# Delta scan of a two-layer block: other orders for block loads, block products, copies and query-decay loads

## What is computed

```python
def gated_delta_chunked(q, k, v, g, beta, s0):
    # S_t = a_t (I - b_t k_t k_t^T) S_{t-1} + b_t k_t v_t^T,  o_t = S_t^T q_t
    ...
    kb = k * beta[..., None]
    m = jnp.where(strict, jnp.einsum('bhnid,bhnjd->bhnij', kb, k) * decay, 0.0)
    a = m + jnp.eye(c, dtype=F32)
    rhs = jnp.concatenate([v * beta[..., None], kb * jnp.exp(g)[..., None]], axis=-1)
    sol = lax.linalg.triangular_solve(a, rhs, left_side=True, lower=True, unit_diagonal=True)
    ...
    def step(s, xs_n):
        v_new = u_n - jnp.einsum('bhck,bhkv->bhcv', w_n, s)
        o_n = jnp.einsum('bhck,bhkv->bhcv', qg_n, s) + jnp.einsum('bhij,bhjv->bhiv', attn_n, v_new)
        s = s * gl_n[..., None, None] + jnp.einsum('bhck,bhcv->bhkv', kd_n, v_new)
        return s, o_n
```

## Time and profile before

| | us |
|---|---|
| median of three runs | 2071.34 (2070.23 to 2074.94) |
| the profiled execution: its own time | 2068.77 |
| the profiled execution: span from the first instruction to the last | 2066.1 |
| TensorE busy | 1891.9 (92% of the span) |
| VectorE busy | 616.7 (30%) |
| ScalarE busy | 431.5 (21%) |
| GpSimd busy | 69.0 (3%) |

### The profile page before, as it was taken

One profiled execution on the slowest core, in us unless ns is written; L12 is line 12 of the kernel. 1 busy time (PEld: TensorE's weight loads), 2 busy tenths in 40 slices (PEclk: granted clock), 3 DMA queues, 4 the chain that ended last, 5 costly groups with the idle time before them and its releaser, 6 DMA issues. The chain is left out here.

```text
span 2066.1 us, 23949 instructions
## 1 busy us (share of the span) xinstructions
PE 1891.9 (92%) x9336; PEld 1040.5 (50%) x9336; DVE 616.7 (30%) x1351; ACT 431.5 (21%) x864; POOL 69.0 (3%) x102
## 2 busy tenths in 40 slices
PE   6999998899999899999899988889999898999997
PEld 3436455896878543332333333323333245767775
DVE  1476555256621211111111111110111223432223
ACT  3222640327231111100111111100111022521011
POOL 1000410100000000000000000000000000000000
PEclk9999999899999899999999999999999999999999
DMA  9444347306383879999999999999999772124442
GB/s 366 163 163 155 141 103 200 87 13 207 83 289 123 346 318 427 428 429 429 428 429 428 429 429 428 429 428 429 428 428 429 304 281 93 62 71 156 149 155 99
DMA packets 97251, 567.12 MB, mean 274 GB/s; under 512 B 32992, under 2 KB 41952, under 8 KB 66080
## 3 DMA queue, kind: packets, MB, share of 16 engines
q1 hardware_dynamic: 94880, 560.69, 68.2%
q10 hardware_dynamic: 2304, 5.51, 0.9%
HBM read 555.02 MB, written 11.14 MB: 274 GB/s over the span
## 5 line engine op out<-in xcount | busy, mean ns | idle before, releaser
L2087 PE MATMUL expert_gb<-expert_ring,hT 128*64 128x512 f32 x768 | 199.7, 598 | 44.6 <-DMA expert_ring<-in_w_gu_units 44.6
L1975 DVE TENSOR_SCALAR hT<-expert_gb 128x512 f32<-128x512 f32 x32 | 22.1, 692 | 682.7 <-PE expert_lb L2087 682.7
L2087 PE MATMUL expert_lb<-expert_ring,hT 128*64 128x512 f32 x768 | 197.4, 592 | 0.0
L2136 PE MATMUL expert_yb<-expert_ring,hT 128*64 128x512 f32 x384 | 167.4, 592 | 0.0
L2136 PE MATMUL expert_yb<-expert_ring,h2T 128*64 128x512 f32 x384 | 167.4, 592 | 0.0
L478 PE MATMUL mix_in_pj<-hT,mix_in_pj_ring 128*128 128x512 f32 (+1 forms) x384 | 143.3, 532 | 1.3 <-DVE hT L598 1.3
L2493 PE MATMUL attend_bank<-hT,expert_ring 128*128 128x256 f32 x640 | 141.4, 379 | 0.0
L2493 PEld LDWEIGHTS attend_bank<-hT,expert_ring 128*128 128x128 f32 x640 | 121.6, 190 | 25.1 <-issue 9.6
L2087 PEld LDWEIGHTS expert_gb<-expert_ring,hT 128*64 128x64 f32 x768 | 51.1, 136 | 155.4 <-DMA expert_ring<-in_w_gu_units 79.4
L2026 ACT ACTIVATE hT<-hT 128x512 f32<-128x512 f32 x32 | 20.2, 631 | 513.2 <-DVE hT L1975 513.2
L150 PE MATMUL delta_scan_fill_bank<-hT,fill_w 128*128 128x512 f32 (+1 forms) x288 | 102.3, 514 | 9.3 <-DMA fill_w<-in_w_fill 6.6
(11 more groups left out here) (483 smaller groups left out, 2589.8 us busy)
## 6 DMA issues: line engine op xcount, KB each, us to landing
expert_ring<-in_w_gu_units SPq DMA_DIRECT2D x96, 2048.0 KB, 29.0
expert_ring<-in_w_down_units SPq DMA_DIRECT2D x48, 2048.0 KB, 32.3
tail<-in_w_gu_units SPq DMA_DIRECT2D x16, 2048.0 KB, 30.5
late<-in_w_gu_units SPq DMA_DIRECT2D x16, 2048.0 KB, 29.0
mix_in_wm<-in_w_mod_units SPq DMA_DIRECT2D x11, 2048.0 KB, 9.4
expert_ring<-in_w_up_units SPq DMA_DIRECT2D x22, 1024.0 KB, 6.2
late<-in_w_down_units SPq DMA_DIRECT2D x8, 2048.0 KB, 34.4
tail<-in_w_down_units SPq DMA_DIRECT2D x8, 2048.0 KB, 35.3
```

The lines of the kernel that those rows point to most:

```text
L1975: v.tensor_scalar(glu, gb[j][:], LIMIT, None, ALU.min).then_inc(s_glu, 1)
L2087: m = pe.matmul(b[halves[h], :], xT[:, k, x], unit[z][:, r0 + c0 + 512 * h:r0 + c0 + 512 * h + 512], start=False, stop=(k == KT - 1))
L2136: m = pe.matmul(yb[h][halves[j], :], hidT[j][:, c, hh * SLOTS:(hh + 1) * SLOTS], unit[z][:, r0:r0 + 512], start=False, stop=(f == 7))
```

## The change

- The mask blocks of direction 1 are stored and loaded back by ScalarE's queue (`store_m(act, 1)` after four of the eight `ktok` copies, `load_m(act, 1)` after all of them); those of direction 0 stay on SP.
- VectorE finishes direction 0 (line 1005, then line 1008) before direction 1.
- The 14 loads of turned blocks get three semaphores per direction and another order: two blocks of `tl` for each direction (`s_x1`), two diagonal blocks of `tt` for each (`s_x2`), then one of `tl` and two of `tt` for each (`s_x3`). y5 waits for the first, d5 for the second, y6 for the third.
- ScalarE issues filler load `f + 2` ahead of copy `f` for products 10 to 15. SP issues loads 18 to 21 and stores 16 to 19 behind the block loads.
- Filler 16 stands behind e5 on TensorE, 17 behind y6, 18 and 19 behind d6.
- e5, y6 and d6 issue one product of direction 0 and one of direction 1 in turn. The lists in `USES` follow.
- The copies of y5 move to VectorE. Those of y6 and d6 are split: ScalarE takes y6 of direction 0 and d6 of direction 1, VectorE the others.
- The two query-decay loads stand ahead of filler store 17 and load 19, after both directions' y6; their Exp stands behind ScalarE's copies of scan step 0.

The diff, cut:

```diff
-    TLB = ((0, 1, 2), (3, 2, 1))
+    TLB = ((0, 2, 1), (3, 1, 2))
+    TTB = ((1, 3, 0, 2), (2, 0, 3, 1))
...
-    for kind in ("y5", "d5", "e5"):
+    for kind in ("y5", "d5"):
         USES += [(kind, d, c) for d in d2 for c in range(2)]
+    USES += [("e5", d, c) for c in range(2) for d in d2]
     for kind in ("y6", "d6"):
-        USES += [(kind, d, t) for d in d2 for t in range(NTILE)]
+        USES += [(kind, d, t) for t in range(NTILE) for d in d2]
...
+        def store_m(eng, d):
+            for g in g2:
+                copied(eng, ("kg", NTILE - 1, g))
+            for b in range(NB):
+                eng.dma_start(A.block_m[d]...[b], tt[d]...[quad(b), :, quad(b)]).then_inc(s_bs[d], 16)
+        def load_m(eng, d):
+            eng.wait_ge(s_bs[d], 16 * NB)
+            eng.dma_start(bm[d]..., A.block_m[d]).then_inc(s_bl, 16)
+        def store_blocks(eng, d):
+            eng.wait_ge(s_sub[d], NSUB + 1)
+            eng.dma_start(A.block_t[d], xt[d]...).then_inc(s_xs[d], 16)
+            eng.wait_ge(s_sub[d], NSUB + 2)
+            eng.dma_start(A.block_tt[d], xx[d]...).then_inc(s_xs[d], 16)
+        def low(eng, d, b, sem):
+            eng.dma_start(tl[d]...[quad(b), :, LC[d, b]:LC[d, b] + BLK], A.block_t[d]...[b]).then_inc(sem, 16)
+        def diagonal(eng, d, b, sem):
+            eng.dma_start(tt[d]...[quad(b), :, quad(b)], A.block_tt[d]...[b]).then_inc(sem, 16)
...
 # SP
                     if f == 5:
-                        (the stores and loads of block_m for both directions)
+                        store_m(sp, 0)
+                        load_m(sp, 0)
-                    if f == 11:
-                        (stores; then for each d four loads into tt, three into tl)
-                for f in range(F1 - 2, F1):
-                    S.fill.store(sp, f)
-                    S.fill.load(sp, f + 2)
+                for d in d2:
+                    store_blocks(sp, d)
+                for d in d2:
+                    sp.wait_ge(s_xs[d], 32)
+                    for b in TLB[d][0:2]:
+                        low(sp, d, b, s_x1[d])
+                for d in d2:
+                    for b in TTB[d][0:2]:
+                        diagonal(sp, d, b, s_x2[d])
+                for d in d2:
+                    low(sp, d, TLB[d][2], s_x3[d])
+                    for b in TTB[d][2:]:
+                        diagonal(sp, d, b, s_x3[d])
+                S.fill.load(sp, 18)
+                S.fill.store(sp, 16)
                 for d in d2:
                     copied(sp, ("y6", d, NTILE - 1))
                     sp.dma_start(qg[d]..., A.decay_rows[d, 2:4]...).then_inc(s_qr[d], 16)
+                for f in range(17, F1):
+                    S.fill.load(sp, f + 2)
+                    S.fill.store(sp, f)
...
 # ScalarE
                 for t in range(NTILE):
+                    if t == 2:
+                        store_m(act, 1)
                     (two copies of ktok)
-                for f in range(6, 18):
+                load_m(act, 1)
+                for f in range(6, 16):
+                    if f >= 10:
+                        S.fill.load(act, f + 2)
                     copy_fill(f)
                     if f >= 10:
                         S.fill.store(act, f)
-                        S.fill.load(act, f + 2)
-                (copies of y5; copy_fill(18))
-                for d in d2:
-                    for c in range(2):
+                for c in range(2):
+                    for d in d2:
                         (copy of e5 (d, c))
-                copy_fill(19)
-                (copies of y6 of both directions; qg: wait and Exp)
+                copy_fill(16)
+                (copies of y6 of direction 0)
+                copy_fill(17)
+                (copies of d6 of direction 1)
+                copy_fill(18)
+                copy_fill(19)
                 for n in range(NTILE):
                     (copies of vn)
+                    if n == 0:
+                        for d in d2:
+                            act.wait_ge(s_qr[d], 16)
+                            act.activation(qg[d], qg[d], ACT.Exp).then_inc(s_qe[d], 1)
...
 # VectorE
                 for d in d2:
                     (line 1005)
-                for d in d2:
                     (line 1008)
+                (copies of y5 of both directions)
                 (copies of d5 of both directions)
-                (copies of d6 of both directions)
+                (copies of y6 of direction 1)
+                (copies of d6 of direction 0)
...
 # TensorE
-                for f in range(6, 18):
+                for f in range(6, 16):
                     fill(f)
                 pe.wait_ge(s_z, 1)
                 for d in d2:
-                    pe.wait_ge(s_xl[d], 16 * (NB + len(TLB[d])))
+                    pe.wait_ge(s_x1[d], 32)
                     (y5)
-                fill(18)
                 for d in d2:
+                    pe.wait_ge(s_x2[d], 32)
                     (d5)
-                for d in d2:
-                    for c in range(2):
-                        (e5 of direction d, half c)
-                fill(19)
+                for c in range(2):
+                    (e5 of both directions, half c, one product of each in turn)
+                fill(16)
                 for d in d2:
+                    pe.wait_ge(s_x3[d], 48)
                     copied(pe, ("e5", d, 1))
-                    (y6 of direction d, four tiles)
+                (y6: four tiles, one product of each direction in turn)
+                fill(17)
                 for d in d2:
                     copied(pe, ("d5", d, 1))
-                    (d6 of direction d, four tiles)
+                (d6: four tiles, one product of each direction in turn)
+                fill(18)
+                fill(19)
```

More of the change, by code:

```diff
@@ L1122, in _ @@
                         m.then_inc(fullsem(("d5", d, c)), 1)
-                for d in d2:
-                    f, x = PAIRS[d][0]
-                    for c in range(2):
-                        take(pe, ("e5", d, c))
-                        for a in range(16 * c, 16 * c + 16):
-                            t, h = a // HA, a % HA
-                            m = pe.matmul(flat(TURN["e5", d, c][0])[quad(x), BLK * (a % 16):BLK * (a % 16) + BLK],
-                                          tt[d][quad(x), t, h, quad(x)], y5s[d][quad(x), a, :], start=True, stop=True)
-                        m.then_inc(fullsem(("e5", d, c)), 1)
@@ L1132, in _ @@
-                fill(19)
-                for d in d2:
-                    copied(pe, ("e5", d, 1))
-                    for t in range(NTILE):
-                        b = take(pe, ("y6", d, t))
-                        for h in range(HA):
-                            m = pe.matmul(flat(TURN["y6", d, t][0])[SECOND[d], 64 * h:64 * h + 64],
-                                          tt[d][FIRST[d], t, h, SECOND[d]], tl[d][FIRST[d], t, h, :], start=True, stop=True)
-                        m.then_inc(fullsem(("y6", d, t)), 1)
+                for c in range(2):
+                    for d in d2:
+                        take(pe, ("e5", d, c))
+                    last = [None, None]
+                    for a in range(16 * c, 16 * c + 16):
+                        t, h = a // HA, a % HA
+                        for d in d2:
+                            f, x = PAIRS[d][0]
+                            last[d] = pe.matmul(flat(TURN["e5", d, c][0])[quad(x), BLK * (a % 16):BLK * (a % 16) + BLK],
+                                                tt[d][quad(x), t, h, quad(x)], y5s[d][quad(x), a, :], start=True, stop=True)
+                    for d in d2:
+                        last[d].then_inc(fullsem(("e5", d, c)), 1)
@@ new lines, in _ @@
+                fill(16)
+                for d in d2:
+                    pe.wait_ge(s_x3[d], 48)
+                    copied(pe, ("e5", d, 1))
+                for t in range(NTILE):
+                    for d in d2:
+                        take(pe, ("y6", d, t))
+                    for h in range(HA):
+                        for d in d2:
+                            last[d] = pe.matmul(flat(TURN["y6", d, t][0])[SECOND[d], 64 * h:64 * h + 64],
+                                                tt[d][FIRST[d], t, h, SECOND[d]], tl[d][FIRST[d], t, h, :], start=True, stop=True)
+                    for d in d2:
+                        last[d].then_inc(fullsem(("y6", d, t)), 1)
```

90 lines of the change are left out of this document (42 added, 48 removed).

## The result

Measured: 2060.23 us (median of 5, 2057.91 to 2062.49) against 2074.94 us for the kernel before beside it (2070.23 to 2077.76). The ratio is 0.9934, 95% interval 0.9919 to 0.9949: faster, by 0.66%. The forecast was 2046 in a range of 2039 to 2058: the measured time lies 14 us above it, outside the range.

The account below looks back on a forecast made before the run. The delta-scan stretch from filler 15 to step 0 was taken as bound by TensorE and its waits. Products 31.2, waits 4 and clock 3 made 38.2 us against 62.40, 24.2 less, giving 2046 us (range 2039 to 2058).

Parts of the forecast that it names:

- The sum's waits and its clock: Filler 15 to step 0: waits 4 us (bounds 1 and 9), clock loss 3 us (0 and 7), beside 31.2 of products.
- The first two land at 342 + 1.8 + 2.6 = 346.4 ... I take 347: Loads ahead of y5: each direction's first two `tl` blocks land at 347, between 346.4 and 350.
- y5 waits beyond 352: Sign at y5's start: waiting past 352 would prove the prediction wrong; y5 was expected at 346 to 349.
- One stretch like the 6.83 us one costs half of it; I take 3: TensorE's clock among the short products: one half-clock stretch costs 3 us, bounds 0 and 7.
- Low clock all along: Rival, y5 to filler 16: clock falls at the first wait and stays down, 6 us more, 2052 us; chance 0.08.
- Mask blocks on two queues: Mask blocks ahead of VectorE's column phase: direction 1 on ScalarE's queue gains 1 us, bounds nothing and 1.4.
- Alternation: e5, y6, d6: alternating directions' corners takes e5 to 1.9 us and halves y6 and d6 from 14.95 to 7.5.
- No overlap: Rival at y6, d6, e5: alternation does nothing for 64x64 corners, 9 us of gain lost, 2055 us; chance 0.12.
- Slower: Rival at y6 and d6: switching corners drains, 218 ns a product, 55.8 us together, total time of 2094 us; chance 0.03.
- Copies on VectorE, filler loads, query decays: y5 copies covered but about 1 us; filler loads hidden; query-decay loads cost 0.5 us wait, their Exp free.
- Loads stay slow: Rival ahead of y6: loads keep 1.8 us each, land at 369, y6 waits 6 to 7 more, 2053 us; chance 0.12.

Follow-up runs that it names:

- the best trace: Changed kernel with mask blocks on SP's queue, `block_t` stored first, filler steps behind y5/d5 halves (three first, two second) and four behind e5: 2046.67 us, 0.9868.

## Why the prediction was wrong, step by step

- **The sum's waits and its clock were wrong, its work somewhat low.** In the best trace, with the clock up and the wait covered, the stretch takes 36.34 us, near the forecast 38.2, but that is luck: it holds 35.08 us of work and 1.26 of idling, where the sum had 31.2 of work, 4 of waits and 3 of clock. By the starts of its rows the short products take 11.4 us there (predicted 9.3), y6 and d6 7.6 (7.5) and the fillers, three of them cut up, 16.1 (14.4).
- **"The first two land at 342 + 1.8 + 2.6 = 346.4 ... I take 347"** failed: y5 starts at 355.65, outside 346.4 to 350; 3.0 us of that are the later last mask product, so it is 5.7 us late (+67.8 against +62.1), and filler 15 ends 2.1 us sooner (+59.3 against +61.4), which lengthens the wait. Only 1.3 of the 5.7 is the issue (+58.4 against +57.1); the rest is the landing, 9.3 us in place of 4.4. The 1.8 us is a mean over 14 loads, and no pace for the first two: in the trace of before too, its first two loads landed 7.5 us behind the first issue (343.83 to 351.30). What shares the engines was shown to count: 3.7 us less idling without two of the filler loads, 3.3 with the `block_tt` stores moved behind, of which 1.8 is the earlier issue. "y5 waits beyond 352" was named as what would prove the prediction wrong, and did.
- **"One stretch like the 6.83 us one costs half of it; I take 3"** failed as a size, and its upper bound of 7 too: 10.6. The rival *Low clock all along* had the mechanism and nearly the numbers (9.3 + 1.9 forecast, 8.6 + 2.05 measured); its 2052 and the 7.5 us of wait that it did not have make 2059.5. It was given 0.08 because d5 had run at full clock for all its 4.05 us, but that was right behind 5.07 us of filler, and the change takes that filler away. That row spoke for the rival as much as against it.
- **The two failed terms do not add up as repairs.** Each repair of the wait alone gave nothing at step 0: the time won went into the stops behind it (d5's 3.64 us, or 2.40 and 1.17) and into filler 16, 0.5 to 0.7 us longer at half clock. With three steps of filler among the short products the earlier loads do reach step 0 (+102.3 against +105.5).
- **Mask blocks on two queues**, a gain of 1 us (0 to 1.4): a loss of about 1.2 at the column phase. The rule quoted there from the Trainium skill, that a second issuing engine saves issue time alone, was nearer than the bound taken from the DMA share.
- **Alternation** was right: y6 and d6 3.95 us each against 3.75, and with directions in turn only by tile the run is 8.8 us slower. *No overlap* and *Slower* are out: 30.9 ns for a 64x64 product (3.95 / 128).
- **Copies on VectorE, filler loads, query decays**: right. No product waits for a copy, fillers 17 to 19 have no wait, y6 has none, and the Exp fills ScalarE's gap, here after:

```profile
399.55 4.23 ACT L939 ACTIVATE delta_scan_r<-delta_scan_bank,tokq 128x128 f32<-128x128 f32 x16 [0.51 <-PE delta_scan_bank L1215]
403.55 3.83 ACT L945 ACTIVATE delta_scan_tl<-delta_scan_tl 128x2048 f32<-128x2048 f32 x2
410.27 4.23 ACT L939 ACTIVATE delta_scan_r<-delta_scan_bank,tokq 128x128 f32<-128x128 f32 x16 [2.89 <-PE delta_scan_bank L1215]
```

*Loads stay slow* is out too: y6 waits for no load, after, where slow products ahead of it help, and in the best run, where they are fast.

Open: no run changes the supply of instructions alone. That it makes the stops among the short products rests on their places in the list and on the packets. What brings the clock down among short products is narrowed and not settled: with two steps, how much of the fall is due to the one stop of 1.09 us and how much to the smaller share of filler was not separated.

## What to carry to other kernels

Price a load by what is in the DMA engines when it is issued, the stores it depends on first, and by its own time from issue to landing, not by the mean pace of a long train of loads. Before large filler products are moved away from a chain of small ones, ask what clock that chain will have: 640 products of 32x32 cost 9.3 us by the full-clock pace and took 17.9 (11.4 in the best run). Where several repairs of one stage each give nothing alone, look for a common limit behind them and try them together with its removal. Where a stop has no named cause, count the instructions between stops: if it stays at its place in the list while the work there changes, the cause is not in that work.

## What the runs showed of the hardware

- TensorE at half clock, busy in 27.31 of 27.31 us with short products and filler mixed; with three steps of filler per half in place of two it kept the full clock over 29.11 us in which it was busy only 25.19.
- Stops of up to 2.28 us within a run of short products, with all operands there. The 31 stops without a load or copy to wait for stand 127 or 128 products, or a multiple, apart, and each ends 1.2 to 1.7 us behind a 16 KB packet on the instruction queue.
- Alternating corners: 64 products of 32x32 listed with 1.20 us at full clock (18.8 ns each) and 1.92 us at half; 128 of 64x64 with 3.95 us, against 7.50 where one corner follows itself.
- A second DMA queue for the mask blocks made their consumer wait 12.63 to 14.30 us (eight traces) in place of 11.81 to 12.38 (six).
